# Block 2's memory keys made behind `w_out`, its values behind `down`; four weight loads get places of their own

## The reference

```
mem_n = rmsnorm_2(mem_2, norm_mem_2)
km, vm = split(mem_n @ w_mem_kv_2)      # keys: first 256 columns, values: last 256
km = rmsnorm_2(km by heads of 64, mem_k_gain)
logits = qm . km / 8 ; out = softmax(logits) @ vm
x = x + concat(o_hg, o_sa, o_mem) @ w_out_2 ; x = x + (silu(a) * b) @ w_ffn_out
```

## Time and profile before

| what | value |
|---|---|
| median of 3 runs | 1625.55 us |
| profiled execution, its own time | 1623.29 us |
| its span | 1621.5 us |
| PE, DVE, ACT, GpSimd busy | 97%, 56%, 39%, 1% |
| mean granted TensorE clock | 0.989 |
| memory traffic | 150 MB, 93 GB/s |

### The profile page before, as it was taken

How to read it: one execution, slowest core, us unless ns; L and a number is a source line. 1 busy time by engine, 2 the same in 40 slices (tenths; PEclk the granted TensorE clock), 3 DMA queues, 4 the chain that set the end, 5 groups by cost and what they waited for, 6 DMA issues and landing times.

```text
span 1621.5 us, 20637 instructions
## 1 busy us (share of the span) xinstructions
PE 1565.8 (97%) x7842; PEld 1309.7 (81%) x7842; DVE 900.9 (56%) x1442; ACT 625.0 (39%) x861; POOL 11.8 (1%) x16
## 2 busy tenths in 40 slices
PE   7999999999998999999999889998899999999999
PEld 7887877888876788888888758998888788888887
DVE  5444476445454777777423767988865434444322
ACT  6441334332233444444323544565563322323211
POOL 0000000000000000000000000000000000000000
PEclk9999999999998999999999999999999999999999
DMA  9312220322222122222422312111002222222222
GB/s 346 124 53 104 76 75 27 110 98 103 104 78 104 39 93 102 103 103 78 155 101 81 119 52 85 72 36 71 27 27 104 80 102 103 94 87 103 104 104 78
DMA packets 25885, 150.24 MB, mean 93 GB/s; under 512 B 2611, under 2 KB 5043, under 8 KB 9436
## 3 DMA queue, kind: packets, MB, share of 16 engines
q1 hardware_dynamic: 25820, 149.35, 25.7%
HBM read 147.21 MB, written 2.13 MB: 92 GB/s over the span
## 4 chain that ended last, share of the span: by engine, by line
PE 84%; DVE 8%; ACT 4%; issue 2%; DMA 1%; SPq 0%; DVEq 0%; ACTq 0%
PE bank L1709 26%; PE bank L1711 25%; PE bank L1710 25%; ACT w_hi L584 2%; PE bank L1823 2%; PE bank L2113 1%; PE bank L1803 1%; PE bank L2050 1%; DVE w_lo L1057 1%; DVE sel L1485 1%; DVE st L1484 1%; DMA x<-xT 1%; PE bank L1812 1%; DMA raw<-weights 1%; DVE w_lo L1065 1%
## 5 line engine op out<-in xcount | busy, mean ns | idle before, releaser
L1709 PE MATMUL bank<-h_hi,w_hi 128*128 128x512 f32 (+1 forms) x1200 | 475.9, 397 | 10.5 <-DVE h_lo L1130 9.2
L1057 DVE TENSOR_TENSOR w_lo<-raw,w_hi 128x2048 fp32r<-128x2048 f32 x118 | 270.3, 2291 | 364.1 <-ACT w_hi L584 363.7
L1711 PE MATMUL bank<-h_hi,w_lo 128*128 128x512 f32 (+1 forms) x1200 | 469.4, 391 | 0.0
L1710 PE MATMUL bank<-h_lo,w_hi 128*128 128x512 f32 (+1 forms) x1200 | 469.1, 391 | 0.0
L584 ACT ACTIVATE w_hi<-raw 128x2048 fp32r<-128x2048 f32 x128 | 244.4, 1910 | 346.4 <-PE bank L1711 344.3
L1709 PEld LDWEIGHTS bank<-h_hi,w_hi 128*128 128x128 f32 (+1 forms) x1200 | 225.7, 188 | 64.8 <-DVE h_lo L1130 9.0
L1711 PEld LDWEIGHTS bank<-h_hi,w_lo 128*128 128x128 f32 (+1 forms) x1200 | 225.6, 188 | 48.9
L1710 PEld LDWEIGHTS bank<-h_lo,w_hi 128*128 128x128 f32 (+1 forms) x1200 | 226.0, 188 | 47.1 <-issue 0.9
L1709 PE MATMUL bank<-a_hi,w_hi 128*128 128x512 f32 x352 | 136.9, 389 | 0.0
L1710 PE MATMUL bank<-a_lo,w_hi 128*128 128x512 f32 x352 | 136.9, 389 | 0.0
L1711 PE MATMUL bank<-a_hi,w_lo 128*128 128x512 f32 x352 | 136.9, 389 | 0.0
(11 more groups left out here) (282 smaller groups left out, 1905.3 us busy)
## 6 DMA issues: line engine op xcount, KB each, us to landing
raw<-weights SPq DMA_DIRECT2D x128, 1024.0 KB, 4.8
toep<-bias_scratch SPq DMA_DIRECT2D x8, 448.0 KB, 4.5
x<-xT SPq DMA_DIRECT2D x2, 1024.0 KB, 9.7
x_tok<-x_tok SPq DMA_DIRECT2D x1, 2048.0 KB, 11.7
outT<-x SPq DMA_DIRECT2D x8, 256.0 KB, 4.4
mem_tok<-mem_tok SPq DMA_DIRECT2D x1, 1024.0 KB, 10.8
mem2T<-mem2T SPq DMA_DIRECT2D x1, 1024.0 KB, 5.7
memT<-memT SPq DMA_DIRECT2D x2, 256.0 KB, 3.7
```

What stands on the lines that cost most here:

```text
L1057: nc.vector.tensor_tensor(w_lo[m % 2][:, :], raw[m % 2][:, :], w_hi[m % 2][:, :].bitcast(F32), ALU.subtract).then_inc(lo_ready, 1)
L1709: nc.tensor.matmul(o, lh, rh, start=first, stop=False)
L1710: nc.tensor.matmul(o, lh, rl, start=False, stop=False)
L1711: return nc.tensor.matmul(o, ll, rh, start=False, stop=last)
```

## The change

1. `mem_kv_2` is cut in two. Its first load (keys) becomes `mem_k2`, between `w_out` and `up`; its second (values) becomes `mem_v2`, in its old place behind `down`. `mem2T` is fetched twice: once while `w_out` runs, for the keys (raised there, low part made there), and again for `down`'s stage as before. The keys' two tiles lie in one bank (6), where they wait for the memory's root, which is still worked out with `down`'s norm; ACT copies them from there to `km_tok` after it.
2. The sums and spreads are issued inside products: the sum after the fifth step of the first key (or value) tile, the spread after the fifth step of the second. The spread takes bank 7.
3. `mem_k2`, `up`'s first load, `mem_v2` and `iq`'s first load have places of their own for high and low part, in space that is free at that time, so they are rounded and split earlier.
4. `together` has a lag as an argument: 0 for `up_first` and `iq` (both loads side by side, 12 products a step), 3 for `up_2_first` as before.
5. A second turn of `up` is written out (`up_second`, banks 0 to 3) with the spread of the norm inside its first tile; the loop has nine turns.
6. Behind `iq`, `iwT` comes before `ik`, with the spread of `x_2` inside it.
7. The masks come as 8-bit numbers straight from memory; the cast on GpSimd is gone. `sel` is cleared after `mem_v2` is used.
8. In the tail the first two `turn_mix` tiles are taken over by ACT and DVE inside the attention loop, and the first two tiles of `w_out_2` (banks 4 and 5) are made step by step between the other turns.

```diff
-LOADS = [... ("w_out", 4), ("up", 22), ("down", 12), ("mem_kv_2", 2), ("iq", 2), ("idx", 1),
+LOADS = [... ("w_out", 4), ("mem_k2", 1), ("up", 22), ("down", 12), ("mem_v2", 1), ("iq", 2), ("idx", 1),
+OWN_PLACE = {FIRST["mem_k2"]: (2, FIRST["w_out"] - 1), FIRST["up"]: (3, FIRST["w_out"]),
+             FIRST["mem_v2"]: (4, FIRST["down"] + 9), FIRST["iq"]: (5, FIRST["down"] + 9)}
...
@@ def plan_banks
     norm("mix")                                  # spread now in bank 7
+    use(("mem_k2", 0), 6, FIRST["mem_k2"])
     together("up_first", FIRST["up"])
     norm("ffn")
-    loop("up", [0, 1, 2, 3], FT // 2 - 1, ...)
+    tiles("up_second", 4, first=FIRST["up"] + 2, per=2)
+    loop("up", [0, 1, 2, 3], FT // 2 - 2, ...)
...
@@ sync
-            stream(FIRST["branch"], FIRST["down"] + 2)
+            stream(FIRST["branch"], FIRST["w_out"] + 2)
+            sp.wait_ge(w_used, FIRST["w_out"])
+            sp.dma_start(mem2T[:, :, :], ...).then_inc(mem2_in, 16)
+            stream(FIRST["w_out"] + 2, FIRST["down"] + 2)
...
@@ scalar
             for m in range(4):
-                round_w(FIRST["w_out"] + m + 1)
+                round_w((FIRST["w_out"] + m + 1) if m < 3 else FIRST["up"] + 1)
+                if m == 2:
+                    round_w(FIRST["mem_k2"])
                 for j in (2 * m, 2 * m + 1):
+                    if j == 5:
+                        round_w(FIRST["up"])
...
+                    if m == 1:
+                        act.wait_ge(mem2_in, 16)
+                        for c in range(4 * (j % 2), 4 * (j % 2) + 4):
+                            raised(mn2_hi[:, c, :], mem2T[:, c, :], "norm_mem_2", c)
...
+                for c in range(2) if g == 3 else ():     # under down
+                    round_w(FIRST["iq"] + c)
...
@@ vector
-            residual("down", out_tile, "g_post_ffn", "norm_mix_2", range(4), between)
-            dve.wait_ge(w_used, FIRST["mem_kv_2"] + 2)
+            residual("down", out_tile, "g_post_ffn", "norm_mix_2", range(4))
+            dve.wait_ge(w_used, FIRST["mem_v2"] + 1)
             residual("down", out_tile, "g_post_ffn", "norm_mix_2", range(4, KT))
+            split_w(FIRST["idx"])
...
@@ tensor
-            norm_sum("mix", S)
-            norm_spread("mix")
-            together("up_first", FIRST["up"], LOW_END["merged"], "ffn")
-            norm_spread("ffn")
+            weights(FIRST["mem_k2"])
+            pe.wait_ge(split, LOW_END["mem_k2"])
+            claim(("mem_k2", 0))
+            for t in range(MT):
+                ins = token_tile(B(("mem_k2", 0))[:, t * M:(t + 1) * M], FIRST["mem_k2"], t, mn2_hi, mn2_lo,
+                                 inside=spread_inside("mix", 4) if t else sum_inside(4, "mix", S))
+            done(("mem_k2", 0), ins)
+            together("up_first", FIRST["up"], LOW_END["mem_k2"], "ffn", 0)
+            for m in range(2):                            # up_second
+                ...    feature_tile(..., inside=spread_inside("ffn", 5) if m + c == 0 else None)
...
-            for m in range(2):                            # mem_kv_2: four tiles, sum and spread between them
-            together("iq", FIRST["iq"], LOW_END["mem_2"], "x_2")
-            norm_spread("x_2")
+            for t in range(MT):                           # mem_v2: two tiles, sum and spread inside
+            together("iq", FIRST["iq"], LOW_END["mem_2"], "x_2", 0)
...
             pe.wait_ge(hg_scaled, TT)
-            for j in range(2, 6):
-                mix_turn(j)
-            all_read("sa", SAH * TT)
-            for j in range(6, KT):
-                mix_turn(j)
-            feature_loads("w_out_2", 4, ...)
+            mix_turn(2)
+            for j in range(3, KT):
+                if j == 6:
+                    all_read("sa", SAH * TT)
+                mix_turn(j)
+                if j < KT - 1:
+                    out_product((j - 3) % 2, (j - 3) // 2)
+            for c in range(2):
+                for kt in range(2, KT):
+                    out_product(c, kt)
...
```

More of the change, by code:

```diff
@@ L109 @@
 IW_SCALE = IDXH ** -0.5 * 64 ** -0.5
+OWN_PLACE = {FIRST["mem_k2"]: (2, FIRST["w_out"] - 1), FIRST["up"]: (3, FIRST["w_out"]),
+             FIRST["mem_v2"]: (4, FIRST["down"] + 9), FIRST["iq"]: (5, FIRST["down"] + 9)}
+PLACE, PREVIOUS = [], []
+for _m in range(NLOADS):
+    _alternate = [_n for _n in range(_m) if _n not in OWN_PLACE]
+    if _m in OWN_PLACE:
+        PLACE.append(OWN_PLACE[_m][0])
+        PREVIOUS.append(OWN_PLACE[_m][1])
+    else:
+        PLACE.append(len(_alternate) % 2)
+        PREVIOUS.append(_alternate[-2] if len(_alternate) > 1 else None)
 class Slot:
@@ L160, in norm @@
         use(("sum", k), 7)
-        use(("spread", k), 6)
+        use(("spread", k), 7)
     def attention(kind, n):
@@ L189, in plan_banks @@
     norm("mix")
+    use(("mem_k2", 0), 6, FIRST["mem_k2"])
     together("up_first", FIRST["up"])
     norm("ffn")
-    loop("up", [0, 1, 2, 3], FT // 2 - 1, {1: FIRST["up"] + 2, 3: FIRST["up"] + 3}, 2)
+    tiles("up_second", 4, first=FIRST["up"] + 2, per=2)
+    loop("up", [0, 1, 2, 3], FT // 2 - 2, {1: FIRST["up"] + 4, 3: FIRST["up"] + 5}, 2)
     loop("down", [0, 1, 2, 3], 2, {1: FIRST["down"] + 2, 3: FIRST["down"] + 5}, 6)
     norm("down")
-    tiles("mem_kv_2", 4, first=FIRST["mem_kv_2"], per=2)
+    tiles("mem_v2", 2, first=FIRST["mem_v2"], per=2)
     together("iq", FIRST["iq"])
     norm("x_2")
-    tiles("ik", 1)
-    use(("iwT", 0), 1, FIRST["idx"])
+    use(("iwT", 0), 1)
+    use(("ik", 0), 0, FIRST["idx"])
     use(("iw", 0), 2)
@@ L219, in plan_banks @@
     tiles("turn_mix", KT)
-    tiles("w_out_2", KT, first=FIRST["w_out_2"], per=2)
+    tiles("w_out_2", KT, (4, 5, 0, 1), first=FIRST["w_out_2"], per=2)
     together("up_2_first", FIRST["up_2"])
@@ L1349, in _ @@
             for m in range(4):
-                split_w(FIRST["w_out"] + m + 1)
+                split_w((FIRST["w_out"] + m + 1) if m < 3 else FIRST["up"] + 1)
+                if m == 2:
+                    split_w(FIRST["mem_k2"])
                 for j in (2 * m, 2 * m + 1):
+                    if j == 5:
+                        split_w(FIRST["up"])
                     add_squares(j == 0)
+                    if m == 1:
+                        for c in range(4 * (j % 2), 4 * (j % 2) + 4):
+                            low_gained(mn2_lo[:, c, :], mem2T[:, c, :], "norm_mem_2", mn2_hi[:, c, :], c)
             norm_scale("mix", S)
-            split_w(FIRST["up"] + 1)
             wait_free(("w_out", KT - 1))
-            residual("mix", lambda j: mixed[:, j, :], "g_post_mix", "g_pre_ffn", range(KT))
+            in_tile = lambda j: mixed[:, j, :]
+            residual("mix", in_tile, "g_post_mix", "g_pre_ffn", range(4))
+            dve.wait_ge(w_used, FIRST["mem_k2"] + 1)
+            residual("mix", in_tile, "g_post_mix", "g_pre_ffn", range(4, KT))
+            split_w(FIRST["up"] + 2)
             norm_scale("ffn", S)
-            split_w(FIRST["up"] + 2)
+            split_w(FIRST["up"] + 3)
             for c in range(2):
@@ L1410, in _ @@
                         add_squares(j == 0, M, ssq_mem)
+                for c in range(2) if g == 3 else ():
+                    split_w(FIRST["iq"] + c)
                 for j in (2 * g, 2 * g + 1):
@@ L1630, in _ @@
                       between=value_gate_tail)
[L1631 to L1632 removed]
+            for j in range(2, KT):
+                if j < 6:
                     low_gained(mo_lo[:, j, :], B(("turn_mix", j))[:, :], "hg_out_gain", mo_hi[:, j, :], 0)
@@ L1733, in token_tile @@
                                   kt == 0, kt == KT - 1)
+                    if inside is not None:
+                        inside(kt)
                 return ins
@@ L1764, in norm_spread, with together @@
                                                         start=True, stop=True))
-            def together(name, first, fresh, norm_name):
-                lag = 3
+            def together(name, first, fresh, norm_name, lag):
                 for step in range(KT + lag):
```

215 lines of the change are left out of this document (125 added, 90 removed).

## The result

The changed kernel takes **1604.6 us** (median of 4 runs, 1603.69 to 1606.16) beside 1625.38 for the kernel before (4 runs, 1624.45 to 1625.95): ratio **0.9876, 95% interval 0.9863 to 0.989**. That is 20.8 us faster. The profiled execution's own time is 1603.69, its span 1601.8, its mean granted clock 0.997 (before 1623.29, 1621.5 and 0.989).

A forecast was written before the change was run, and what follows sets the result against it. PE bounds the kernel, busy 1565.8 of 1621.5 us; only its idle places and low clock can be won. Gains 4.9 + 11.8 + 1.6 = 18.3, less 1.5 for clock, is 16.8: 1625.55 to 1608.8 us, range 1605.7 to 1614.9.

The forecast's parts named there:

- Norm behind `w_out`: Between `w_out` and `up_second`: key products cover sum and spread, leaving a gap of 2.3 us; gain 4.9 us.
- The sign that was named: From `w_out`'s last product to the end of the second pair of `up` loads: falls from 61.2 to near 56.3 us.
- Norm behind `down`: From `down`'s end to the first indexer product: gain 11.8 us, of which 5.75 is products moved away.
- Rival 4: At both norms DVE's tiles, not PE, set the pace; most moved keys return as waiting: 1614.5 us, chance 4%.
- The `up` loop: DVE's split ends at 569.7 for a PE that asks at 571.1: hidden, by 1.4 us.
- rival 3: A rounding or split of `up` or `up+4` comes one fetch late, losing about 3.4: 1612.2 us, chance 10%.
- The tail: `mix` turns with twelve `w_out_2` products between them: gain 1.6 us, bounds 0 and 2.2.
- The clock: One short low-clock stretch behind each of the two norms, about 0.75 us each: 1.5 us off the gain.
- the base: Timed median of the kernel before, 1625.55 us, from which the gain was subtracted; its profiled execution took 1623.29.
- Outside these, PE is fed: Claim that PE's idle places are the gaps around the norms behind `w_out` and `down`; no size given.
- no low stretch: Rival: the clock stays high in both norms, gain 18.3 us, 1607.3 us, chance 17%.

The follow-up runs named there:

- e6: Changed kernel with 42 of the 48 key products behind `w_out` left out, sum and spread on their own again: 1605.6 us.
- e7: Changed kernel with `iq`'s two loads rounded and split between the residual tiles behind `down` again, and lag 3 for `iq` alone: 1613.87 us.
- e4: Changed kernel with the lag of three steps back in both `up_first` and `iq`: 1612.52 us.
- e9: Changed kernel with the 48 value products behind `down` issued twice: 1607.4 us.
- e3: Changed kernel with the tail of before, all `mix` turns ahead of `w_out_2`'s products: 1606.07 us.
- e2: Changed kernel run again with no edit: 1604.28 us, ratio 0.9872 to the kernel before.
- e10: Changed kernel with only ACT's rounding of `hf`'s load moved ahead of the memory keys' head norms: 1602.04 us.
- e12: Changed kernel run a third time with no edit: 1604.77 us, ratio 0.9871 to the kernel before.
- e1: Kernel before the change run again with no edit: 1624.58 us over 11 runs.
- e11: Changed kernel with only the two spreads issued after the third step of the second tile, not the fifth: 1602.94 us.
- e8: Changed kernel with `hf`'s load rounded earlier on ACT and both spreads issued after the third step instead of the fifth: 1599.71 us.

## Why the prediction was wrong in size

**Norm behind `w_out`: right.** 4.88 measured from `w_out`'s last product (4.74 in the table), 4.9 forecast, each position within 0.35. The sign that was named is there: from that product to the end of the second pair of `up` loads it is 56.4 (514.95 to 571.31), 56.3 forecast. e6 shows the claim behind it: the keys lie in holes that would otherwise stand empty.

**Norm behind `down`: right as a sum (11.62 for 11.8), for reasons that the forecast did not part.** Counted from the end of `down`, each position lies within 0.3 of the forecast: the first `iq` step at 10.30 (10.3), the second at 13.97 (14.0), the next sum at 33.19 (33.0), the indexer at 50.22 (50.0). But it said "of which 5.75 is the products moved away". The runs give another account of the same stage:

| kernel | stage behind `down`, us | step |
|---|---|---|
| before | 61.84 | |
| e7, splits between and lag 3, keys moved | 59.96 | -1.88: keys moved, sum and spread inside, `iwT` first |
| e4, splits ahead, lag 3 | 54.24 | -5.72: no splits between DVE's tiles |
| after, lag 0 | 50.22 | -4.02: both loads open together |

Moving 5.75 us of products out brought about 2 (1.88 here, 2.30 the other way round in e9). The splits and the lag brought 9.7, in this order of the steps; the 5.72 of the splits includes what the low clock between them cost in e7's profile. Rival 4 feared exactly this for the products, but took it that nothing would come in its place.

**The `up` loop: right.** DVE's first turn starts at 554.64 (forecast 554.3), and the split that was given 1.4 us of slack ends at 570.07:
```profile
554.64 1.29 DVE L1206 TENSOR_TENSOR tap<-bank,rms 128x512 f32<-128x512 f32 x2
...
567.78 2.29 DVE L1094 TENSOR_TENSOR w_lo<-raw,w_hi 128x2048 fp32r<-128x2048 f32 x1 [1.11 <-ACT w_hi L605]
```
PE has no wait for a weight in the loop, so rival 3 did not come.

**The tail: mis-sized.** 1.6 forecast, 2.21 in the positions (1.7 by e3's). I counted three pairs of turns at 1.04 and 0.2 for changing over; a turn between products takes PE only 0.35 (1191.45 to 1191.80), the change included.

**The clock: the step that failed.** The prediction put it as "I take one such stretch in each: 18.3 - 1.5 = 16.8", at 0.75 a norm. Both the number and the price were too high, and this is the largest single term of the miss: 1.5 of 4.2. In the seven profiled executions whose first norm has the 2.21 gap and 12 products a step (after, e2, e3, e7, e9, e10, e12), the clock over 525 to 535 was 1.00 three times and 0.83 to 0.85 four times. Behind `down`, in the six with that gap (after, e2, e3, e6, e10, e12), it was 1.00 every time. So a low stretch came in 4 of 13 places, not in each. And it costs 0.5: from the first step to the next sum it is 22.89 in after (525.03 to 547.92) and 23.38 in e12 (528.22 to 551.60), since the second step waits for DVE anyway; the other two executions with a high clock there take 22.89 and 22.90 (e7, e2), the other three with a low one 23.36 to 23.45 (e9, e3, e10). That makes 0.3 where 1.5 was taken off. The row that misled was the 2.08 gap before 910.34: the gap was as long, but the splits that stood between DVE's tiles came behind it too; e7 brings them back and has the low clock there, but its first wait is longer too, 4.65. Which of the two, gap or later waits, decides is not parted by these runs; that stays open.

**What the sum left out.** The low stretch at the indexer's start is shorter (0.63 gained up to the tail, in e2 and e12 as well). The 0.5 at the end lies behind the last arithmetic: DVE's last addition starts 343.9 behind the sum in before and after alike, and from the issue of the last output transfer to the end of the span it is 2.8 in before (1618.66 to 1621.5) and 2.4 in after (1599.45 to 1601.8). It repeats in e1, e2 and e12, but e3 and e4, whose code is the same there, have 3.7 and 3.5. So it is no work of the change that I can name, and what sets it is open.

**The account.** Positions: 16.8 + 1.5 (clock) + 0.6 (tail) + 0.6 (indexer) + 0.5 (end) - 0.3 (the two norms' small misses) = 19.7. The remaining 1.35 of the 4.2 us miss is the base, which is luck and no mechanism: the profiled run of before lay 2.26 under the median that I subtracted from, that of after 0.91 under its own. Over all rounds the changed kernel's 12 runs have a median of 1604.45, and before lies between 1624.5 and 1625.4.

The prediction's "Outside these, PE is fed" was too strong: in before PE also waits 7.3 for `w_lo`, all of it in the first 13 us, and 6.3 for `mix` in the attention units. These waits stayed (8.6 and 6.5 after), so the sum doesn't suffer by it.

**The range** failed because of more than that step: with no low stretch at all the forecast would have been 1607.3, which it holds. Its near side held "no low stretch" (1607.3) and 1.6 beyond, but not that case together with a tail at its bound and fewer low stretches elsewhere: 18.3 + 0.6 + 0.6 + 0.5 is 20, which is 1605.6, just outside; less the 0.3 of the two norms and with the 1.35 of the base it is about 1604.5. The range was built as if each of the small terms could only be lost.

The Trainium skill (TensorE: Matmul & The Clock Gate, Part 1: The HAM clock gate) says that the monitor runs free of the kernel, so that the count of slow matmuls differs from run to run. The runs agree: one and the same gap of 2.21 us was followed by a high clock in e2 and a low one in e12. The prediction named this rule, gave 17% to no low stretch, and still took the low stretch as certain in its sum.

## What to carry to other kernels

Price a clock term as a chance times a cost, and take the cost after what the waits behind it absorb: a low stretch in front of a step that waits for another engine cost 0.5 us here, not half its length. Independent products moved into a hole are free up to the size of the hole (e6, e9; in e9 the hole took up 3.4 us where its idle time was 2.9), but what shortens a stage is more often what stands between the tiles of the engine that sets its pace: 5.7 us for two weight splits with the low clock between them, 4.0 for a lag. When all bounds of a sum are listed, ask for each small term what it would be if it went better than planned, and put the range there too.

## What the runs showed of the hardware

**Run time follows the mean granted clock in the changed kernel.** The 12 runs of the changed kernel: five at mean clock 0.994 take 1606.1 us on average, six at 0.996 to 0.998 take 1603.5. For the kernel before it is no such clean order (e1). The places vary from run to run: e12's profile has 0.83 at the first norm, after's 1.00.

**A DVE copy took longer beside a GpSimd memset.** This is where e11's gain behind `down` went. The copy of `square` into `ssq` takes 0.42 in after, where it starts 0.05 behind the end of GpSimd's memset of `sel`; in e11 it starts 0.67 before that end and takes 0.96, ending 0.29 behind it. e8, with the same early spread, shows the same (0.95). At the first norm, where no memset runs, the copy takes 0.42 in all of these. After:
```profile
895.27 1.81 POOL L565 MEMSET sel<- 128x2048 f32 x1 [785.62 <-PE bank L1756]
```
```profile
897.13 0.42 DVE L1113 COPY ssq<-square 128x512 f32<-128x512 f32 x1
897.46 0.74 DVE L1175 SCALAR_TENSOR_TENSOR down<-down,vec,bank 128x512 f32<-128x512 f32 x1
```
e11:
```profile
895.45 1.81 POOL L565 MEMSET sel<- 128x2048 f32 x1 [786.25 <-PE bank L1756]
```
```profile
896.59 0.96 DVE L1113 COPY ssq<-square 128x512 f32<-128x512 f32 x1
897.46 0.73 DVE L1175 SCALAR_TENSOR_TENSOR down<-down,vec,bank 128x512 f32<-128x512 f32 x1
```
The next tile starts at 897.46 in both. The Trainium skill (SBUF — State Buffer, Terms) describes this as a port pair that DVE and GpSimd take one at a time, the loser standing still; the traces of e8 and e11 agree for this copy, in that it ends only behind the memset; spans on GpSimd are rough. In e9 the memset comes later (902.63), behind the copy (898.72), and the copy takes 0.42. The early spread with a later memset was not tried.
